# Hybrid decoder block: state blocks in pairs, four C products instead of two, normalised rows scaled later, parameters loaded as rows

## The chip, the cores and the metric

One core of a Trainium2 chip runs the whole program. The metric is the device time of one launch in microseconds (us). Engines are named as in the profile: PE (matrix engine; PEld its weight loads), DVE (vector), ACT (scalar), POOL (GpSimd), SP (sync, here only a DMA queue).

## The reference

One layer on 512 positions of width 1024. What matters here is the beginning:

```python
h = layer_norm(x, ln_in_g, ln_in_b)
proj = h @ w_in[l]
u, q, k, v, q_idx, k_idx, w_idx, gate_pre = jnp.split(proj, split_points, axis=-1)
...
dt = jnp.exp(log_dt)[:, None];  a_bar = jnp.exp(lam * dt)            # lam complex
bu = einsum('blgp,gnp->blgn', u, ((a_bar - 1.0) / lam)[..., None] * b_c)
_, states = lax.associative_scan(combine, (a_seq, bu), axis=1)       # s_t = a_bar s_(t-1) + bu_t
y = einsum('blgn,gpn->blgp', states, c_c).real + d_skip * u          # then GELU and a GLU
```

There are 32 groups of 16 channels with 64 complex states each. Beside this branch runs a sparse attention (an indexer picks 128 keys for each query, 8 heads). Both are gated and projected, added to the scaled h and normalised; then come the top 4 of 32 experts and a last normalisation.

## The kernel before

Each engine has a program of its own, written out by hand, and waits on semaphores; nothing is reordered. The time goes through these stages: a start (parameters and x are loaded, x is normalised and transposed), the first projection tiles, 16 state blocks on DVE with the other projection tiles on PE beside them, the indexer with its top-128 selection and the gates, the attention with the GLU, the output projection and the router, and the expert loop, which is about two thirds of the time.

**The start.** SP issues the loads of x (L379) and the weights of u (`chunk(0)`), then the small weights and `chunk(1)`. ACT's queue issues the parameters as columns, one number for each partition (L647 to L656), in its program *ahead of* the square roots of the first norm (L660); more parameters follow behind the square roots (L664 to L670). DVE normalises the four row tiles one after the other (L950 to L955, `norm`), PE transposes them (L1381), and ACT scales and shifts the transposed tiles into `hT` (L676). ACT and DVE then work out the coefficients of the states from `sp_in` (L680 to L686, L966 to L1003), and PE transposes the B and C blocks (L1432, L1439).

**Projection tiles.** A tile (`tile`, L1388 to L1420) is 8 fp32 matmuls of 512 columns, which the profile shows as 16 instructions (two passes each), into the PSUM banks 0 and 1 in turn; ACT takes it (`take`, L733). The four u tiles are done before the state blocks begin, 17 others (4 qi, ki, 4 q, 4 k, 4 v) beside them.

**State blocks.** Block j holds 128 states (two groups). For each of the 16: PE multiplies u by B into banks 2 and 3 (`bu`, L1452, contraction over 32 rows); ACT and POOL make the phase (`phase_products` on ACT, L475 to L486 on POOL) and ACT its sine and cosine (`trigs`, L702 to L704); DVE (`s5`, L1024 to L1049) rotates (4 products from PSUM, 2 sums), scans twice (L1037, L1038) and rotates back (4 products, L1044 and L1048 the difference and the sum) into `w_st`; PE multiplies by C (`ymm`, L1461, 32 output rows). Both `phase` and `w_st` have two buffers. Every fourth block DVE adds the skip term (`y_out`, L1055).

**What stands around it.** After the phases POOL multiplies and adds ln_in's rows to h (L504, L505: 8 instructions of 128x1024), which first the residual sum behind the output projection needs (semaphore `s_hrow`). Behind the last state block PE works out the indexer's head weights (L1481, semaphore `s_wi`), for which POOL and DVE wait before they split `hT` (L519, L1075); with these the gate tiles begin (L1494). In the attention POOL splits the GLU weights (L549, L551), and later w_o's (L558).

## Time and profile before

| | us |
|---|---|
| median of 3 runs | 1899.23 (1895.12 to 1900.89) |
| profiled execution, device time | 1896.33 |
| its span | 1894.5 |
| busy in the span: PE, DVE, ACT, POOL | 1712.5, 1550.2, 1078.5, 531.7 |
| share of PE on the chain that ended last | 72% |
| share of DVE on that chain | 18% |

Read the table with care: busy shares are means over stages with different limits. The chain of waits, followed in order of time, is what says who is last in each stage, and the table of busy times by stage says how full the others are. A PE instruction's duration holds its fill and drain; back to back matmuls overlap, so stretches are told from start to start.

### The profile page before, as it was taken

What the parts mean: (1) busy time and instruction counts of PE and PEld (TensorE: products, weight loads), DVE (VectorE), ACT (ScalarE), POOL (GpSimd) and SP (SyncE); (2) the same over time, 40 slices, a digit from 0 to 9 for tenths busy, and PEclk for the clock granted to TensorE, in tenths of its full rate; (3) what the DMA queues carried; (4) which work ended last, traced back from release to release, by engine and by line L of the source; (5) the groups of instructions that cost most, each with busy time, mean ns of one, the idle gap of its engine ahead of it and who ended that gap; (6) DMA issues with size and microseconds to landing.
All of it is one profiled execution on the core that took longest, in us unless ns stands there. A gap on an engine that the chain in (4) does not pass through costs nothing.

```text
span 1894.5 us, 22584 instructions
## 1 busy us (share of the span) xinstructions
PE 1712.5 (90%) x7162; PEld 1143.8 (60%) x7162; DVE 1550.2 (82%) x1738; ACT 1078.5 (57%) x1030; POOL 531.7 (28%) x310
## 2 busy tenths in 40 slices
PE   0899887798999768999999999999999999999992
PEld 0433333576666635777777777777777777777761
DVE  1399997794446777999999999999999999999993
ACT  0332321334544525777777777777777777777770
POOL 0165554435206235222222222222222222222220
PEclk9998997899999858999999999999999999999996
DMA  5120111112112366999999999999999999999973
GB/s 151 37 75 14 45 45 45 45 45 89 45 57 78 109 227 258 351 364 359 386 362 364 379 364 361 376 363 361 381 361 359 380 365 356 381 369 362 379 276 103
DMA packets 103796, 465.44 MB, mean 246 GB/s; under 512 B 33184, under 2 KB 33232, under 8 KB 54512
## 3 DMA queue, kind: packets, MB, share of 16 engines
q1 hardware_dynamic: 74064, 441.92, 61.1%
q0 software_dynamic: 9424, 16.86, 3.9%
q10 hardware_dynamic: 20272, 6.23, 1.4%
q8 instruction: 18, 0.29, 0.1%
q14 instruction: 18, 0.15, 0.0%
HBM read 454.81 MB, written 18.92 MB: 250 GB/s over the span
## 4 chain that ended last, share of the span: by engine, by line
PE 72%; DVE 18%; ACT 3%; issue 3%; ACTq 2%; POOL 1%; DMA 1%; DVEq 0%; POOLq 0%
PE ps L1668 19%; PE ps L1670 18%; PE ps L1669 18%; PE ps L1654 2%; PE ps L1419 2%; PE ps L1676 2%; PE ps L1414 2%; DVE scr L1037 1%; DVE scr L1038 1%; DVE scr L1093 1%; DVE top L1092 1%; DVE scr L1035 1%; PE ps L1524 1%; DVE scr L1034 1%; DVE scr L1042 1%
## 5 line engine op out<-in xcount | busy, mean ns | idle before, releaser
L1171 DVE TENSOR_TENSOR w_lo<-raw,w_hi 128x2048 fp32r<-128x2048 f32 x384 | 873.3, 2287 | 81.2 <-ACT w_hi L839 81.2
L839 ACT ACTIVATE w_hi<-raw 128x2048 fp32r<-128x2048 f32 x384 | 736.2, 1918 | 241.8 <-PE ps L1670 241.8
L1668 PE MATMUL ps<-w_hi,x_hi 128*96 128x512 f32 x1024 | 414.8, 405 | 0.0
L1669 PE MATMUL ps<-w_hi,x_lo 128*96 128x512 f32 x1024 | 402.8, 393 | 0.0
L1670 PE MATMUL ps<-w_lo,x_hi 128*96 128x512 f32 x1024 | 402.8, 393 | 0.0
L604 POOL DMA_INDIRECT gate_now<-gate_rows,row_now x32 | 80.2, 2506 | 468.7 <-DVE tok_out L1299 448.2
L1668 PE MATMUL ps<-w_hi,a_hi 128*96 128x512 f32 x512 | 204.2, 399 | 5.7 <-DVE a_lo L1270 5.7
L1670 PEld LDWEIGHTS ps<-w_lo,x_hi 128*96 128x96 f32 x1024 | 166.0, 162 | 70.9
L1668 PEld LDWEIGHTS ps<-w_hi,x_hi 128*96 128x96 f32 x1024 | 168.7, 165 | 65.6 <-issue 0.4
L1669 PEld LDWEIGHTS ps<-w_hi,x_lo 128*96 128x96 f32 x1024 | 166.6, 163 | 63.7
L1670 PE MATMUL ps<-w_lo,a_hi 128*96 128x512 f32 x512 | 202.2, 395 | 0.0
L1669 PE MATMUL ps<-w_hi,a_lo 128*96 128x512 f32 x512 | 201.7, 394 | 0.0
L612 POOL DMA_INDIRECT sum_rows<-far,tok_out x32 | 77.9, 2435 | 367.2 <-ACT far L927 367.2
L1419 PE MATMUL ps<-ring 128*128 128x512 f32 x256 | 126.5, 653 | 1.0 <-ACT ring L676 1.0
L1668 PEld LDWEIGHTS ps<-w_hi,a_hi 128*96 128x96 f32 x512 | 83.1, 162 | 39.3 <-issue 5.8
L1670 PEld LDWEIGHTS ps<-w_lo,a_hi 128*96 128x96 f32 x512 | 83.1, 162 | 36.2
L1669 PEld LDWEIGHTS ps<-w_hi,a_lo 128*96 128x96 f32 x512 | 83.3, 163 | 33.9
L1419 PEld LDWEIGHTS ps<-ring 128*128 128x128 f32 x256 | 52.5, 210 | 74.1 <-issue 72.7
L596 POOL DMA_INDIRECT scr<-h_rows,tok_now x33 | 72.1, 2184 | 80.4 <-DVE tok_now L1293 74.7
L1110 DVE SCALAR_TENSOR_TENSOR scr<-far,ps 128x128 f32<-128x128 f32 (+3 forms) x32 | 15.6, 488 | 62.9 <-PE ps L1524 61.8
L927 ACT ACTIVATE far<-ps,gate_now 96x512 f32<-96x512 f32 x64 | 40.3, 679 | 43.5 <-PE ps L1670 43.5
L1494 PE MATMUL ps<-hT_hi,wg_hi 128*128 128x512 f32 x128 | 52.1, 407 | 9.1 <-POOL wg_lo L515 9.1
(296 smaller groups left out, 2335.4 us busy)
## 6 DMA issues: line engine op xcount, KB each, us to landing
raw<-in_w_up SPq DMA_DIRECT2D x256, 1024.0 KB
raw<-in_w_down SPq DMA_DIRECT2D x128, 1024.0 KB
ring<-in_w_in SPq DMA_DIRECT2D x9, 2048.0 KB, 7.8
ring<-in_w_glu SPq DMA_DIRECT2D x4, 1024.0 KB, 6.2
ring<-in_w_o SPq DMA_DIRECT2D x2, 2048.0 KB, 11.9
h<-in_x SPq DMA_DIRECT2D x4, 512.0 KB, 5.6
ring<-in_w_attn_proj SPq DMA_DIRECT2D x1, 2048.0 KB, 9.1
h_rows<-h ACTq DMA_DIRECT2D x4, 512.0 KB
```

Source lines behind the costliest of these rows:

```text
L596: g.indirect_dma_start(xg[:, :], None, h1_rows, bass.IndirectOffsetOnAxis(ap=tok_now[:, 0:1], axis=0), bounds_check=last_tok, oob_is_err=F ...
L604: g.indirect_dma_start(gate_now[:, :], None, gate_rows, bass.IndirectOffsetOnAxis(ap=row_now[:, 0:1], axis=0), bounds_check=last_row, oob_ ...
L612: g.indirect_dma_start(sum_rows, bass.IndirectOffsetOnAxis(ap=tok_out[:, 0:1], axis=0), ysb.rearrange("p a b -> p (a b)"), None, bounds_ch ...
L839: s.activation(hi_of(c)[:, :], raw_of(c), ACT.Copy).then_inc(s_hi, 1)
L927: s.activation(ysb[:, r, :], ps[4 + r][0:BLK, :], ACT.Copy, scale=gate_now[:, 0:1]).then_inc(s_ysb, 1)
L1171: d.tensor_tensor(lo_of(c)[:, :], raw_of(c), hi_of(c)[:, :], ALU.subtract).then_inc(s_lo, 1)
L1414: ins = mm(o[:, :], w[:, k, P * i:P * i + P], qiT[:, k, :], start=k == 0, stop=k == 3)
L1419: ins = mm(o[:, :], w[:, k, c:c + P], hT[:, k, :], start=k == 0, stop=k == KD - 1)
L1494: mm(ps[n % 2][:, :], wg_hi[:, g % 2, k, :], hT_hi[:, k, :], start=k == 0, stop=False)
L1668: mm(o, xh, hi_of(c)[:, col], start=start, stop=False)
L1669: mm(o, xl, hi_of(c)[:, col], start=False, stop=False)
L1670: return mm(o, xh, lo_of(c)[:, col], start=False, stop=stop)
```

## The change

Four things change. (1) The parameters of one number for each partition are loaded as rows into `ptin` (84 rows of 128), spread by DVE for log_dt, transposed once by PE and copied to `ptab` by ACT. The loads of B, C, ln_in's rows and the router go from ACT's queue to SP's, behind `chunk(0)` and `chunk(1)`. The norm's measuring of tile t goes ahead of the shifting of tile t-1. (2) Only one u tile is made before the state blocks, three go into the stream of tiles beside them (20 tiles instead of 17). (3) `bu` and `ymm` take two blocks at a time, which lie in different groups of 32 rows (`bu`, four PSUM banks) or 32 output rows (`ymm`); `s5` leaves out the difference and the sum, and `ymm` multiplies the four products by C, -C' and so on, four matmuls for a block instead of two. `phase` has four buffers, `w_st` three. (4) POOL's 8 instructions on h go from behind the phases to behind the split of the GLU weights.

```diff
+        trig = scr[:, 0:4].rearrange("p (b r) t -> p b r t", b=2)
+        m = scr[:, 4:8]
+        phase, whole = v, ring[:, 4, 3136:3648]
+        part_lo = sb("part_lo", [P, SEQ])
+        rest = [ring[:, 5, 3584:4096], part_lo[:, :]]
+        w_st = [scr[:, 8:12], scr[:, 12:16], ring[:, 5, 1536:3584].rearrange("p (k t) -> p k t", k=4)]
...
+            for r, nm in enumerate(("b_re", "b_im")):
+                sp.dma_start(braw[:, r], a[nm][0].rearrange("(j w) n c -> (w n) j c", w=2)).then_inc(s_par[1], 16)
+            for r, nm in enumerate(("c_re", "c_im")):
+                src = a[nm][0].rearrange("(q g) c n -> (g c) q n", q=4)
+                for dup in range(2):
+                    sp.dma_start(craw[:, r, :, 64 * dup:64 * dup + 64], src).then_inc(s_par[2], 16)
...
+                if n == 1:
+                    for r, nm in enumerate(("ln_in_g", "ln_in_b")):
+                        sp.dma_start(gb[:, r, :], a[nm].partition_broadcast(P)).then_inc(s_gb1, 16)
+                    sp.dma_start(w_rt[:, :, :], a["w_router"][0].rearrange("(k p) n -> p k n", p=P)).then_inc(s_par[3], 16)
+                    sp.dma_start(b_rt[:, :], a["b_router"][0].partition_broadcast(P)).then_inc(s_par[3], 16)
...
-            pool.wait_ge(s_gb1, 32)
-            pool.wait_ge(s_lnT, KD)
-            for t in range(TT):
-                step(g.tensor_tensor(h[:, t, :], h[:, t, :], gb[:, 0, :], ALU.mult))
-                g.tensor_tensor(h[:, t, :], h[:, t, :], gb[:, 1, :], ALU.add).then_inc(s_hrow, 1)
-                pool.wait_ge(s_hrow, t + 1)
...
+            pool.wait_ge(s_gb1, 32)
+            pool.wait_ge(s_lnT, KD)
+            for t in range(TT):
...
+            for row, src in ((0, a["lam_re"][0].rearrange("(j w) n -> j (w n)", w=2)),
+                             (SJ, a["lam_im"][0].rearrange("(j w) n -> j (w n)", w=2)),
+                             (R_LN, a["ln_in_g"].rearrange("(k p) -> k p", p=P)),
+                             (R_LN + KD, a["ln_in_b"].rearrange("(k p) -> k p", p=P)),
+                             (R_GATE, a["b_gate"][0].rearrange("(k p) -> k p", p=P)),
+                             (R_SKIP, a["d_skip"][0].rearrange("(q g) c -> q (g c)", q=4))):
+                act.dma_start(ptin[row:row + src.shape[0], :], src).then_inc(s_ptl, 16)
+            act.dma_start(ldt[2 * SJ:3 * SJ, :], a["log_dt"][0].rearrange("(j w) -> j w", w=2)).then_inc(s_ptl, 16)
+            act.wait_ge(s_ptT, 1)
+            s.activation(ptab[:, :], ps[2][:, 0:NPAR], ACT.Copy).then_inc(s_ptab, 1)
...
+            act.wait_ge(s_ptab, 1)
+            s.activation(spw[:, 0, :], sp_in[:, 2, :], ACT.Exp).then_inc(s_dt, 1)
+            act.wait_ge(s_th, 1)
+            s.activation(spw[:, 2, :], spw[:, 1, :], ACT.Exp).then_inc(s_dt, 1)
             for k in range(KD):
                 act.wait_ge(s_lnT, k + 1)
                 s.activation(hT[:, k, :], ps[4 + k % 4][:, :], ACT.Identity, scale=gbc[:, 0, k:k + 1],
                              bias=gbc[:, 1, k:k + 1]).then_inc(s_hT, 1)
 
...
             def phase_products(j):
-                if j >= 1:
-                    act.wait_ge(s_ph, j)
                 if j >= 2:
-                    act.wait_ge(s_phfree, j - 1)
-                s.activation(phase[:, j % 2, :], tcol[:, :], ACT.Copy, scale=spw[:, 21, j:j + 1]).then_inc(s_prod, 1)
-                s.activation(turn[:, 1, :], tcol[:, :], ACT.Copy, scale=spw[:, 22, j:j + 1]).then_inc(s_prod, 1)
+                    act.wait_ge(s_ph, j - 1)
+                if j >= 4:
+                    act.wait_ge(s_phfree, j - 3)
+                s.activation(phase[:, j % 4, :], tcol[:, :], ACT.Copy, scale=spw[:, 21, j:j + 1]).then_inc(s_prod, 1)
+                s.activation(rest[j % 2], tcol[:, :], ACT.Copy, scale=spw[:, 22, j:j + 1]).then_inc(s_prod, 1)
             def trigs(j):
-                if j + 1 < SJ:
-                    phase_products(j + 1)
+                if j + 3 < SJ:
+                    phase_products(j + 3)
                 act.wait_ge(s_ph, j + 1)
                 if j >= 2:
-                    act.wait_ge(s_rot, j - 1)
-                s.activation(trig[:, j % 2, 1, :], phase[:, j % 2, :], ACT.Sin, scale=TWO_PI).then_inc(s_trig, 1)
-                step(s.activation(trig[:, j % 2, 0, :], phase[:, j % 2, :], ACT.Abs))
+                    act.wait_ge(s_st, j - 1)
+                s.activation(trig[:, j % 2, 1, :], phase[:, j % 4, :], ACT.Sin, scale=TWO_PI).then_inc(s_trig, 1)
...
+            act.wait_ge(s_tau, 1)
+            act.wait_ge(s_const, 2)
+            phase_products(0)
+            phase_products(1)
+            take(n)
+            n += 1
+            phase_products(2)
+            for q in range(8):
+                act.wait_ge(s_bbT, q + 1)
+                r, qq = q // 4, q % 4
+                s.activation(bT[:, r, qq, :], ps[4 + q % 4][:, 0:P], ACT.Copy).then_inc(s_bT, 1)
...
+            def measure(t):
+                dve.wait_ge(s_x[t], 16)
+                for r in range(2):
+                    step(d.bn_stats(stats[:, r, :], h[:, t, 512 * r:512 * r + 512]))
+                d.bn_aggr(mvx[:, t, :], stats[:, :, :]).then_inc(s_var, 1)
+                dve.wait_ge(s_var, t + 1)
+
+            def shift(t):
+                dve.wait_ge(s_rstd, t + 1)
+                step(d.reciprocal(rsx[:, t, 1:2], rsx[:, t, 0:1]))
+                d.tensor_scalar(h[:, t, :], h[:, t, :], mvx[:, t, 0:1], rsx[:, t, 1:2], ALU.subtract, ALU.mult)\
+                    .then_inc(s_xhat, 1)
+
+            dve.wait_ge(s_ptl, 7 * 16)
+            d.tensor_copy(ptin[2 * SJ:3 * SJ, :].rearrange("j (w n) -> j w n", w=2),
+                          ldt[2 * SJ:3 * SJ, :].unsqueeze(2).to_broadcast([SJ, 2, STATES])).then_inc(s_ptx, 1)
             for t in range(TT):
-                dve.wait_ge(s_x[t], 16)
-                norm(h[:, t, :], t + 1, step).then_inc(s_xhat, 1)
-                dve.wait_ge(s_xhat, t + 1)
+                measure(t)
+                if t > 0:
+                    shift(t - 1)
+            shift(TT - 1)
...
-                if j >= 2:
-                    dve.wait_ge(s_stfree, j - 1)
-                wr, w_im = w_st[:, j % 2, 0, :], w_st[:, j % 2, 1, :]
-                step(d.tensor_tensor(m[:, 0, :], m[:, 1, :], c, ALU.mult))
-                step(d.tensor_tensor(m[:, 2, :], m[:, 3, :], sn, ALU.mult))
-                step(d.tensor_tensor(wr, m[:, 0, :], m[:, 2, :], ALU.subtract))
-                step(d.tensor_tensor(m[:, 0, :], m[:, 1, :], sn, ALU.mult))
-                d.tensor_tensor(m[:, 2, :], m[:, 3, :], c, ALU.mult).then_inc(s_rot, 1)
-                dve.wait_ge(s_rot, j + 1)
-                d.tensor_tensor(w_im, m[:, 0, :], m[:, 2, :], ALU.add).then_inc(s_st, 1)
+                if j >= 3:
+                    dve.wait_ge(s_stfree, (j - 3) // 2 + 1)
+                w = w_st[j % 3]
+                step(d.tensor_tensor(w[:, 0, :], m[:, 1, :], c, ALU.mult))
+                step(d.tensor_tensor(w[:, 1, :], m[:, 3, :], sn, ALU.mult))
+                step(d.tensor_tensor(w[:, 2, :], m[:, 1, :], sn, ALU.mult))
+                d.tensor_tensor(w[:, 3, :], m[:, 3, :], c, ALU.mult).then_inc(s_st, 1)
                 dve.wait_ge(s_st, j + 1)
 
             def y_out(q):
-                dve.wait_ge(s_stfree, 4 * q + 4)
...
+            pe.wait_ge(s_ptx, 1)
+            tr(ps[2][:, 0:NPAR], ptin[0:NPAR, :], ident[0:NPAR, 0:NPAR]).then_inc(s_ptT, 1)
...
-            def bu(j):
-                rows = slice(32 * (j % 4), 32 * (j % 4) + 32)
-                if j >= 1:
-                    pe.wait_ge(s_bufree, j)
+            def bu(p):
+                if p % 2 == 0:
+                    pe.wait_ge(s_tile_a, p // 2 + 1)
+                if p >= 1:
+                    pe.wait_ge(s_bufree, 2 * p)
                 for r in range(2):
-                    ins = mm(ps[2 + r][:, :], bT[rows, r, j // 4, :], uT[rows, j // 4, :], start=True, stop=True)
+                    for j in (2 * p, 2 * p + 1):
+                        rows = slice(32 * (j % 4), 32 * (j % 4) + 32)
+                        ins = mm(ps[2 + 4 * (j % 2) + r][:, :], bT[rows, r, j // 4, :], uT[rows, j // 4, :], start=True,
+                                 stop=True)
                 ins.then_inc(s_bu, 1)
-            def ymm(j):
-                q, rows = j // 4, slice(32 * (j % 4), 32 * (j % 4) + 32)
-                pe.wait_ge(s_st, j + 1)
-                if j % 4 == 0 and q > 1:
+            def ymm(p):
+                q = p // 2
+                pe.wait_ge(s_st, 2 * p + 2)
+                if p % 2 == 0 and q > 1:
                     pe.wait_ge(s_yfree, q - 1)
-                for r in range(2):
-                    ins = mm(ps[5 - q % 2][rows, :], cblk[:, r, j, :], w_st[:, j % 2, r, :], start=r == 0, stop=r == 1)
+                for k, r in enumerate((0, 2, 1, 1)):
+                    for j in (2 * p, 2 * p + 1):
+                        rows = slice(32 * (j % 4), 32 * (j % 4) + 32)
+                        ins = mm(ps[5 - q % 2][rows, :], cblk[:, r, j, :], w_st[j % 3][:, k, :], start=k == 0, stop=k == 3)
                 ins.then_inc(s_stfree, 1)
-            order = [(1, 4), ("small", 1), (2, 4), (3, 4), (4, 4)]
-            flat = [(c, i == cnt - 1) for c, cnt in order for i in range(cnt)]
-            for j, (c, last) in enumerate(flat):
-                if j < SJ:
-                    bu(j)
+            order = [(0, 3), (1, 4), ("small", 1), (2, 4), (3, 4), (4, 4)]
+            flat = [c for c, cnt in order for i in range(cnt)]
+            bu(0)
+            for i, c in enumerate(flat):
                 if c == "small":
                     pe.wait_ge(s_small, 32)
-                elif c != (flat[j - 1][0] if j else None):
+                elif c != (flat[i - 1] if i else 0):
                     arrive(c)
                 tile(n, c if c != "small" else 0)
                 n += 1
-                if 1 <= j <= SJ:
-                    ymm(j - 1)
+                if i % 2 == 0 and 1 <= i // 2 <= SJ // 2:
+                    ymm(i // 2 - 1)
+                if i % 2 == 1 and i // 2 + 1 < SJ // 2:
+                    bu(i // 2 + 1)
+            pe.wait_ge(s_bufree, SJ)
```

## Rows read from the trace of the kernel before

**Rows 1.** Stages: length; PE, PEld, DVE, ACT, POOL busy; granted clock; DMA; GB/s

```profile
0.00:38.70 38.70, 0.00 (x0) 0.00 (x0) 1.74 (x6) 0.00 (x0) 1.84 (x8) 1.00 0.67 179
...
38.70:61.60 22.90, 8.12 (x33) 6.47 (x33) 8.69 (x17) 7.96 (x14) 0.00 (x0) 1.00 0.44 86
...
61.60:97.60 36.00, 35.27 (x86) 16.01 (x87) 12.12 (x41) 11.64 (x26) 9.23 (x9) 0.99 0.08 24
...
97.60:281.70 184.10, 167.44 (x346) 61.70 (x345) 177.47 (x197) 50.06 (x84) 104.23 (x83) 0.94 0.12 41
...
281.70:304.40 22.70, 13.31 (x27) 4.20 (x25) 22.32 (x13) 2.95 (x5) 22.09 (x8) 0.87 0.00 1
...
319.10:339.70 20.60, 14.01 (x76) 11.08 (x77) 11.30 (x11) 6.94 (x7) 9.59 (x4) 0.66 0.29 102
...
455.50:564.70 109.20, 102.44 (x507) 75.76 (x507) 49.41 (x114) 57.24 (x120) 27.96 (x29) 0.97 0.13 46
```

**Rows 2.** Start in order of time (start, duration, engine)

```profile
38.73 1.28 ACT L660 ACT_TABLE_LOAD   x1 [38.73 <-issue]
...
40.35 0.16 DVE L953 RECIPROCAL rstd<-rstd 128x1 f32<-128x1 f32 x1 [34.50 <-ACT rstd L660]
...
43.42 0.16 DVE L953 RECIPROCAL rstd<-rstd 128x1 f32<-128x1 f32 x1 [0.36 <-ACT rstd L660]
...
53.84 0.53 ACTq L668 DMA_DIRECT2D gb<-in_ln_in_g  x1
```

**Rows 3.** DMA issues until 100 us: KB each, us to landing

```profile
ring<-in_w_in SPq DMA_DIRECT2D x3, 2048.0 KB, 12.7
...
h<-in_x SPq DMA_DIRECT2D x4, 512.0 KB, 5.6
...
bgate<-in_b_gate ACTq DMA_DIRECT2D x1, 8.0 KB, 3.6
```

**Rows 4.** Last normalised tile to first state block, in time order

```profile
49.77 0.81 DVE L955 TENSOR_SCALAR h<-h,mv,rstd 128x1024 f32<-128x1024 f32 x1
...
56.08 5.46 ACT L676 ACTIVATE ring<-ps,gbc 128x512 f32<-128x512 f32 x8 [6.55 <-issue]
...
61.59 16.32 PE L1419 MATMUL ps<-ring 128*128 128x512 f32 x32 [1.00 <-ACT ring L676]
...
65.59 0.20 DVE L980 TENSOR_TENSOR spw<-spw 128x16 f32<-128x16 f32 x1 [0.21 <-ACT spw L686]
...
74.52 0.91 DVE L1009 MEMSET ring<- 128x1024 f32 x1 [0.28 <-issue]
...
97.60 0.69 DVE L1029 TENSOR_TENSOR scr<-ps,scr 128x512 f32<-128x512 f32 x1 [17.36 <-ACT scr L704]
```

**Rows 5.** DVE groups, first 14 state blocks: count, busy us, mean ns

```profile
L1037 DVE TENSOR_TENSOR_SCAN scr<-spw,scr 128x512 f32<-128x512 f32 x14 | 22.0, 1572 | 0.5
...
L1044 DVE TENSOR_TENSOR scr<-scr 128x512 f32<-128x512 f32 x14 | 10.6, 760 | 0.5
...
L1029 DVE TENSOR_TENSOR scr<-ps,scr 128x512 f32<-128x512 f32 x14 | 9.7, 691 | 17.7 <-ACT scr L704 17.4
```

**Rows 6.** A scan without POOL beside it, on DVE

```profile
312.22 1.22 DVE L1037 TENSOR_TENSOR_SCAN scr<-spw,scr 128x512 f32<-128x512 f32 x1
```

**Rows 7.** PE and its weight loads (PEld), in order of time

```profile
117.90 7.13 PE L1419 MATMUL ps<-ring 128*128 128x512 f32 x16
...
319.12 1.90 PE L1461 MATMUL ps<-scr,ring 128*32 128x512 f32 x4 [0.26 <-DVE scr L1048]
...
319.57 0.11 PEld L1461 LDWEIGHTS ps<-scr,ring 128*32 128x32 f32 x1 [0.32 <-issue]
...
320.95 9.53 PE L1481 MATMUL ps<-ring 128*128 128x8 f32 x64
...
346.81 0.70 PE L1507 MATMUL ps<-kiT,qiT 64*128 64x256 f32 x4
```

**Rows 8.** POOL between the GLU weights and w_o, in order of time

```profile
568.63 2.61 POOL L558 TENSOR_TENSOR wo_lo<-ring,wo_hi 128x512 fp32r<-128x512 f32 x2 [67.04 <-ACT wo_hi L830]
```

More of the change, by code:

```diff
@@ L478, in _ @@
                 tau = spw[:, 20, j:j + 1]
[L479 to L480 removed]
+                f, r = phase[:, j % 4, :], whole
+                lo = rest[j % 2]
                 step(g.tensor_scalar(r, tcol[:, :], tau, ROUND, ALU.mult, ALU.add))
@@ L1443, in _ @@
-            pe.wait_ge(*taken[n - 1])
+            tile(n, 0)
+            n += 1
+            pe.wait_ge(s_par[2], 64)
+            for r in range(2):
+                for q in range(4):
+                    tr(ps[2 + r][:, P * q:P * q + P], craw[:, r, q, :], ident[:, :]).then_inc(s_cT, 1)
+            pe.wait_ge(s_bb, 1)
+            for q in range(8):
+                r, qq = q // 4, q % 4
+                if q >= 4:
+                    pe.wait_ge(s_bT, q - 3)
+                tr(ps[4 + q % 4][:, 0:P], bblk[:, r, 4 * qq:4 * qq + 4, :].rearrange("p j c -> p (j c)"), ident[:, :])\
+                    .then_inc(s_bbT, 1)
```

107 lines of the change are left out of this document (29 added, 78 removed).

## Prediction

> **What bounds the kernel now.** I read the table of stages first, then the chain of waits in order of time, then the timelines where the chain changes engine. Of the 1894.5 us the change touches the first 340 and one place in the attention. In those 340 there are four stages.
>
> From 0 to 38.7 nothing computes: PE, DVE and ACT are busy 0, 1.74 and 0 us [rows 1]. ACT's queue is issuing DMAs, and the square root stands behind them in ACT's program, so that even its table load begins at 38.73. DVE waited 34.5 us for the root [rows 2]. x was there long before (5.6 us to landing) [rows 3].
>
> From 38.7 to 97.6 the path is: four norm tiles on DVE, the transposes, then ACT, which came to the first `hT` tile at 56.08 only, since its queue was issuing again; two u tiles on PE in 16.32 us; B and C; two more u tiles; and the first state block at 97.60, for which DVE waited 17.36 us [rows 4]. PE is busy 35.27 of 36.0 us from 61.6 on [rows 1].
>
> From 97.6 to 319.1 the chain is DVE's: 177.47 busy of 184.1 us for the first 14 blocks, the rest the gaps between instructions [rows 1]. PE is nearly as full, 167.44, but waits for DVE. From 281.7 to 304.4 POOL's 8 instructions on h run (22.09 us busy), and DVE gets only 13 instructions done in 22.7 us [rows 1].
>
> From 319.1 on: the last C product 1.90 us, the indexer's weights 9.53 us on PE, and at 330.5 POOL and DVE begin to split `hT` [rows 7]. From there to the attention the change alters no instruction. I take 330.5 as the post at which the stages are compared.
>
> **Part 1, the start.** ACT's queue now issues 7 DMAs of a few long rows. Neighbours of few large pieces cost it 0.53 us each [rows 2], so 7 x 0.53 = 3.7, and the last is issued at 4.5. To landing: 3.6 us in a quiet queue for bgate, 5.6 for x's 512 KB [rows 3]. I take 3.8, nearer the first since the pieces are small: 8.3. The ends are 7 and 15.5, the latter if the rows wait until u's weights are in (issued at 2.8, 12.7 to landing) [rows 3]. DVE, which waits for these rows ahead of its first norm, has behind it: the spreading, 0.3 (estimate), and four norm tiles. The distance of two reciprocals is 3.07, of which 0.36 is the wait for the root [rows 2], which measuring ahead hides: 4 x 2.7 = 10.8. The last tile is normalised at 19.4. PE's transpose of the parameters and ACT's copy lie inside that.
>
> Before, the last tile was normalised at 50.6 [rows 4] and the eight `hT` tiles ended at 61.5, held up by ACT. Without that hold PE's transposes set the pace: 32 of them and a first one kept PE busy for 8.12 us [rows 1], and all but the first three stand behind the last normalised tile: 29 x 0.246 = 7.1, and ACT's last copy 0.5 (5.46 for 8 [rows 4], partly beside it). `hT` is ready at 27. Now two strands run. PE: the first u tile takes 16.32 - 7.1 = 9.2 (the second runs at 7.1 [rows 7], the first partly at half the rate) and ends at 36.4. DVE: from the sines to the B blocks 65.6 to 74.3, 8.7 us [rows 4]; the sines come behind `hT` with a table load of 1.28 and 0.7 us of small work: 27 + 2.0 + 8.7 = 37.7. Then C's blocks: a clearing of 1.5 times 0.91 [rows 4], six copies at 0.45: 42 with a little contention, and C's transposes are done by then. The B products of the first pair, 2 to 2.5 us: DVE starts block 0 at 45. The phases are ready a little before, at 44: ACT's products at 31, two turns of POOL at 5 to 6 us each, then cosine and sine. B, C and the small weights, now on SP's queue behind `chunk(0)`, hold up nothing: SP computes nothing, `chunk(1)` behind them is needed at 70, and B at 33. **97.6 to 45 is 52.6 us less**; range 48 to 57.
>
> **Part 2, the state blocks.** A product of two tiles takes 691 ns [rows 5], and the gap behind each instruction is (184.1 - 177.47) / 197 = 0.034 [rows 1]: 0.726. A scan alone takes 1.22, so 1.26 [rows 6]. A block by itself: 12 x 0.726 + 2.52 = 11.2. Measured: 184.1 us for 14 blocks and two skip terms, less one instruction, so 13.1. The 1.85 between is POOL's doing: the scans' mean is 1572 ns here, the sum's 760, while products that read PSUM keep 691 [rows 5]. The new block has 10 instead of 12: 16 x (10 x 0.726 + 2.52) = 156.5. POOL's work on the phases stays; some 14 of 16 phases fall beside the blocks: 14 x 1.85 = 25.9. Three skip terms, 2.3. Together 184.7 against 221.5: **36.8 us less**, of which 23.2 are the 32 instructions left out and 12 the removal of POOL's work on h. Does PE keep up? For a pair: 2 tiles 14.3, `bu`, `ymm`. Two matmuls of 64 rows each in different row groups, four passes of 256 columns, took 0.70 us [rows 7]; one after the other four such passes would be 4 x 0.21 + 0.27 = 1.1 (a tile's 16 passes of 512 columns take 7.13, 0.43 to 0.45 each [rows 7]). So row groups do run side by side here, and `bu` costs about 2. For output column groups no row of the trace shows it. `ymm` has 16 passes: 3.7 if pairs overlap, 7.0 if not (4 took 1.90 [rows 7]). PE then has 20.0 or 23.3 at full clock against DVE's 184.7 / 8 = 23.1. Granted clock was 0.94 [rows 1], which makes the tiles some 0.5 to 0.8 longer: 21.3 or 24.6. I take the overlapping, by the nearest row. `bu` of the next pair may be 4 us late before DVE notices, since six instructions of the last block run on behind its release. End of block 15: 45 + 184.7 = 229.7, ends 181 and 198 for the stage.
>
> The Trainium skill ("TensorE: Matmul & The Clock Gate", Part 3: Packing small matmuls) states a measured speedup of 2.38 for three column groups of 32 at 512 columns; by it two would take hardly more than one, an estimate of 3.7 to 4.2 for `ymm`. The same part says that a weight load overlaps a running matmul only when the row groups differ, which speaks against `ymm`, where they are the same. The trace disagrees: L1461's weight loads (0.11 us) fall into the stretch of its four matmuls, and these took no longer than passes of a tile, 4 x 0.43 and a drain [rows 7]. By the rule a pair would cost 16 x 0.11 = 1.8 us more on PE, which the slack above just holds.
>
> **Part 3, what comes back behind the blocks.** Before, `ymm` of the last block and the weights followed at once. Now the stream has 20 tiles, and three of them stand behind the last `ymm` in PE's program. PE can't do them earlier, as it waits there for DVE. Behind block 15: 3.7 + 3 x 7.13 + 9.53 = 34.7 against 11.4 [rows 7], and 1 for a clock that falls while PE waits: **24 us more**, ends 22 and 28. ACT's copy of `hT` waits for the last of these tiles too, but its 3.6 us lie beside the 9.53. So of the 23 us that the three u tiles saved ahead of the blocks, the tail takes nearly all back.
>
> **Part 4, POOL's work on h.** It moves to where POOL was idle for 67.04 us [rows 8]; about 22 us fit in ahead of w_o, and neither ACT's nor DVE's wait on `s_hrow` is last there. DVE is busy 49.41 of 109.2 us in this stage and PE 102.44 [rows 1], so what POOL slows on DVE is mostly hidden. One instruction in twelve there reads two tiles of SBUF, and could take 2 us longer, two or three times: 0 to 5, I take 1. On SP's and ACT's queues nothing else is moved past a wait.
>
> **The sum.** The profiled execution took 1896.33, its span 1894.5, and it lies 2.9 below the median. -52.6 - 36.8 + 24 + 1 = -64.4, so 1832 for an execution like the profiled one, and 1834.8 from the median 1899.23. I give 1834.
>
> **Rivals.** (A) Column groups don't overlap, so the change does not do that part of what it says. PE needs 24.6 us for a pair against 23.1: 8 x 1.5 = 12, and 3.3 at the tail, and as PE no longer waits there is no slack for slow tiles: 3 more. 1852. For it: no row shows column groups. Against: row groups do overlap. Chance 0.12. (B) The clock falls more often: PE now waits in one piece a pair, with the small `bu` behind it; in the stage where it waited most before (13.31 busy of 22.7 us) the granted clock was 0.87 against 0.94 [rows 1]. With tiles of 10 a pair takes 25.7: 8 x 2.6 = 21. 1855. Against: a slower PE waits less, which brings the clock back. 0.13. (C) The parameter rows land only with u's weights at 15.5: +7, 1841. 0.10. (D) Slower than before: PE stays at the lower of its two levels, 1.2 GHz, through the blocks, as it was most of the time from 319.1 to 339.7 (0.66 [rows 1]). Tiles of 14.3, `bu` and `ymm` doubled: 40 us for a pair, 8 x 17 = 136, and 25 at the tail: 1995. It decides once a tile is x longer with 8 x (2x - 3.1) + 3x = 65, where 3.1 is PE's slack in a pair and 65 my gain: x = 4.7, a tile of 11.9. The granted clock of 0.94 with PE busy for 91% of the stage [rows 1] speaks against it. 0.03. (E) POOL's phases, made ahead, disturb DVE half as much: 13 less, 1821. 0.04.
>
> **How the numbers follow.** My forecast has 0.58: 1824 to 1845 by its own bounds. C and E lie at its rim. A and B reach to 1856. 1820 to 1857 leaves out D and some of A and B, under 2 in 10. 0.3% (5.7 us) is about what a measurement of this kernel tells from no change; only D is slower: faster 0.96, same 0.01, slower 0.03.
>
> **What would show it.** The first square root at about 10 us and block 0 at 45: part 1. DVE without waits from there to 230 and ten instructions a block: part 2; waits of DVE for `bu` mean A or B, and `ymm` of 3.7 or 7.0 us tells which. Three v tiles between the last `ymm` and L1481's successor: part 3. The attention within 5 us of 109: part 4. Wrong would make it a wait that I don't see between the pairs, or a start that hangs on B's landing.

## The result, and the profile of the changed kernel

| | before | after |
|---|---|---|
| median, us (4 runs each, same chip) | 1900.06 (1895.12 to 1904.45) | 1841.82 (1839.94 to 1844.39) |
| ratio, with its 95% interval | | 0.9691 (0.9673 to 0.9709) |
| profiled execution; its span | 1896.33; 1894.5 | 1839.94; 1838.2 |

The kernel is 3.1% faster, some 58 us. The forecast was 1834, from 1820 to 1857. The time lies inside, 8 us above the likeliest value. The stages of the two profiled executions show where these 8 come from.

One line from the top of the changed kernel's page (busy time, share of the span and instructions of each engine):

```profile
PE 1696.1 (92%) x7227; PEld 1139.8 (62%) x7227; DVE 1519.6 (83%) x1709; ACT 1081.0 (59%) x1032; POOL 524.9 (29%) x310
```

Its stages, cut where the work changes (columns as in [rows 1]: length; PE, PEld, DVE, ACT, POOL busy; granted clock; DMA share; GB/s). They are the start until ACT's first square root, the rest of the start, the state blocks, what PE does behind them, the gap before the gate tiles, the first 6.1 us of the gate tiles, and the attention. The rest of the gate tiles (285.0 to 393.6) and all behind 506.6 are left out:

```profile
0.00:10.97 10.97, 0.37 (x1) 0.18 (x1) 2.33 (x8) 2.81 (x4) 1.84 (x8) 1.00 0.84 317
10.97:49.70 38.73, 19.83 (x73) 11.62 (x73) 26.13 (x60) 19.49 (x39) 21.25 (x20) 0.86 0.51 140
49.70:232.00 182.30, 167.94 (x436) 64.27 (x437) 173.21 (x195) 50.60 (x85) 88.43 (x72) 0.94 0.12 42
232.00:269.70 37.70, 37.70 (x136) 22.01 (x134) 2.20 (x9) 7.78 (x7) 0.61 (x1) 0.88 0.22 79
269.70:278.90 9.20, 2.60 (x9) 1.19 (x9) 9.13 (x4) 1.04 (x3) 9.01 (x3) 0.50 0.00 1
278.90:285.00 6.10, 6.10 (x15) 4.81 (x16) 3.08 (x3) 1.67 (x2) 2.35 (x1) 0.51 0.00 0
393.60:506.60 113.00, 103.62 (x513) 76.31 (x512) 53.24 (x120) 59.99 (x125) 49.78 (x40) 0.97 0.14 48
```

[rows 1] cuts the attention of the kernel before at 455.5. From the same instruction as here, its first matmul (L1524 before, L1552 now), it is:

```profile
452.50:564.70 112.20, 103.28 (x513) 76.27 (x512) 50.85 (x120) 60.09 (x125) 30.49 (x32) 0.97 0.14 49
```

Set against [rows 1], with the attention cut in this way, this gives the account of the span. The start takes 49.7 instead of 97.6 us (-47.9, forecast -52.6), the blocks 182.3 instead of 221.5 (-39.2, forecast -36.8), and from the last block to the split of `hT` it takes 37.7 instead of 11.5 (+26.2, forecast +24). From the split of `hT` to the attention it takes 1.9 more, the attention 0.8 more (forecast 1), and what follows 1.8 more, which is less than single executions differ by. The sum is -56.4. The spans differ by 56.3.

**The start**, DVE in order of time:

```profile
8.64 0.22 DVE L979 COPY ptin<-ldt 16x128 f32<-16x128 f32 x1 [7.58 <-DMA ldt<-in_log_dt]
...
18.65 0.81 DVE L975 TENSOR_SCALAR h<-h,mvx,rsx 128x1024 f32<-128x1024 f32 x1
...
29.40 1.10 DVE L1012 TENSOR_TENSOR spw<-spw,ptab 128x16 f32<-128x16 f32 x1
30.54 0.17 DVE L1013 TENSOR_TENSOR spw<-spw,ptab 128x16 f32<-128x16 f32 x1
...
34.83 0.42 DVE L1023 TENSOR_TENSOR scr<-spw,far 128x256 f32<-128x256 f32 x1
35.29 1.37 DVE L1024 TENSOR_TENSOR scr<-spw,far 128x256 f32<-128x256 f32 x1
...
49.73 0.69 DVE L1053 TENSOR_TENSOR scr<-ps,scr 128x512 f32<-128x512 f32 x1 [3.98 <-PE ps L1474]
```

Three things are to be seen. The wait for the last parameter row ends at 8.64; before, 34.5 us went to waiting for the root [rows 2]. Instructions of one form last 0.17 or 1.10 us, and 0.42 or 1.37. Block 0 waits for PE at the end. PE in the same stretch:

```profile
25.91 7.13 PE L1441 MATMUL ps<-ring 128*128 128x512 f32 x16 [1.81 <-ACT ring L688]
...
41.34 1.97 PE L1459 MATMUL ps<-ident,far 128*128 128x128 f32 x8 [7.43 <-DVE far L1027]
45.85 3.78 PE L1474 MATMUL ps<-uT,ring 32*128 32x512 f32 x8 [2.54 <-issue]
```

PE stands for 7.43 us in front of the B blocks and then does the first B products in 3.78 us, at a granted clock of 0.50 (1.2 GHz) from 45.8 to 49.6. The second pair, at 65.06 with a granted clock of 1.00, takes 1.99.

**The blocks**, DVE by groups (count | busy us, mean ns | idle before). The products that read PSUM kept their 691 ns; what reads two tiles of SBUF, and the scans, take longer on the mean than alone (0.69 and 1.22 us):

```profile
L1062 DVE TENSOR_TENSOR_SCAN scr<-spw,scr 128x512 f32<-128x512 f32 x16 | 23.5, 1466 | 0.6
L1061 DVE TENSOR_TENSOR_SCAN scr<-spw,scr 128x512 f32<-128x512 f32 x16 | 21.4, 1335 | 0.5
L1058 DVE TENSOR_TENSOR scr<-scr 128x512 f32<-128x512 f32 x16 | 13.7, 859 | 0.5
...
L1054 DVE TENSOR_TENSOR scr<-ps,scr 128x512 f32<-128x512 f32 x16 | 11.1, 691 | 0.5
```

The waits of PE in the blocks (us in total, times, longest):

```profile
PE ps L1474 <- DVE scr L1056: 12.8, 5, 4.0
```

And the first passes of the C products of a pair of blocks on PE, in order of time. The two blocks write different column groups, each its own 32 of the 128 output rows (`ring` and `scr` are their two `w` buffers):

```profile
101.41 0.62 PE L1487 MATMUL ps<-ring 128*32 128x512 f32 x1
101.42 0.62 PE L1487 MATMUL ps<-scr,ring 128*32 128x512 f32 x1
101.87 0.59 PE L1487 MATMUL ps<-ring 128*32 128x512 f32 x1
...
104.97 5.42 PE L1441 MATMUL ps<-ring 128*128 128x512 f32 x12
```

Both passes of a pair start within 0.01 us, the next pair 0.43 later, and the next tile starts 3.56 us behind the first: `ymm` costs 3.6, as forecast for column groups side by side.

**Behind the blocks**, PE:

```profile
234.10 0.62 PE L1487 MATMUL ps<-ring 128*32 128x512 f32 x1
...
237.66 20.87 PE L1422 MATMUL ps<-ring 128*128 128x512 f32 x48
258.36 11.28 PE L1509 MATMUL ps<-ring 128*128 128x8 f32 x64
```

Three tiles stand between `ymm` and the indexer's weights, as forecast.

### The profile page after: what moved, and what is told of

The parts are those of the page before. It is cut to its first block, busy times and chain, and to the rows that moved or that the text cites. A ratio compares the mean times of both kernels' runs of the same rounds, so it can differ in the third digit from the quotient of the medians.

```text
span 1838.2 us, 22681 instructions
## 1 busy us (share of the span) xinstructions
PE 1696.1 (92%) x7227; PEld 1139.8 (62%) x7227; DVE 1519.6 (83%) x1709; ACT 1081.0 (59%) x1032; POOL 524.9 (29%) x310
## 4 chain that ended last, share of the span: by engine, by line
PE 77%; DVE 14%; issue 3%; ACT 3%; DMA 1%; POOL 1%; ACTq 0%; DVEq 0%; POOLq 0%
PE ps L1696 19%; PE ps L1698 19%; PE ps L1697 19%; PE ps L1682 3%; PE ps L1441 2%; PE ps L1704 2%; PE ps L1436 2%; PE ps L1422 2%; DVE scr L1112 1%; DVE top L1111 1%; DVE scr L1062 1%; PE ps L1552 1%; PE ps L1430 1%; DVE scr L1061 1%; PE ps L1571 1%
```

## The experiments

All are the changed kernel with one edit, unless said otherwise; ratios are to the kernel before on the same chip. The runs used three chips, on which the kernel before took 1897.9 (e1 to e4), 1904.2 (e5, e7 to e9) and 1902.5 us (e10, e11), so a difference of a few us between two medians is better read from the ratios. My theory has four parts. The start is worth its 48 us, most of it from the way in which the parameters are loaded. The blocks gain by shorter work of DVE, whose instructions POOL stretches. Column groups overlap, but PE's share is slack. And the u tiles saved ahead of the blocks return behind them.

### e1: POOL's scaling of h back beside the blocks

```
 # POOL, ahead of  pool.wait_ge(s_far0, 1)
+            pool.wait_ge(s_gb1, 32)
+            pool.wait_ge(s_lnT, KD)
+            for t in range(TT):
+                step(g.tensor_tensor(h[:, t, :], h[:, t, :], gb[:, 0, :], ALU.mult))
+                g.tensor_tensor(h[:, t, :], h[:, t, :], gb[:, 1, :], ALU.add).then_inc(s_hrow, 1)
+                pool.wait_ge(s_hrow, t + 1)
 # and the same lines taken out beside the attention
```

> The changed kernel with POOL's 8 instructions on h put back behind the phases, beside the last state blocks. My theory: they cost DVE 12 us there and about 1 in the attention, so 11 us more than the changed kernel's 1842: 1853, and DVE's scans beside them take over 3 us. Rival: PE, not DVE, sets the end of the last blocks by now, which swallows most of it: 1845 or less. Second rival: in the attention they cost as much as in the blocks: 1842.

1855.01 us (1854.19 to 1857.08), ratio 0.9763 (0.9733 to 0.9794). The blocks (columns as in the stages above):

```profile
51.30:248.39 197.09, 174.41 (x432) 66.53 (x433) 187.05 (x195) 50.72 (x85) 109.22 (x80) 0.87 0.10 35
```

The same 195 instructions of DVE are busy for 13.8 us more than in the changed kernel (173.2), while POOL works 20.8 us more beside them, and the stage is 14.8 longer. The place of POOL's work is worth 13 us of the whole. How it comes about is seen where one scan stands beside it; the first line is POOL's, the second DVE's:

```profile
202.53 2.68 POOL L525 TENSOR_TENSOR h<-h,gb 128x1024 f32<-128x1024 f32 x1
203.03 3.26 DVE L1061 TENSOR_TENSOR_SCAN scr<-spw,scr 128x512 f32<-128x512 f32 x1
```

While POOL's last five instructions on h follow each other, from 202.5 to 217.1, DVE gets five instructions done, of 2.65 to 3.26 us each (alone 0.69 or 1.22), about one for each of POOL's. What it costs beside the attention can't be read: the attention takes 115.6 us here, without POOL's work on h in it, 113.0 in the changed kernel, and 112.4 to 116.1 in the traces of the other experiments, all of which have it there.

### e2: two C products, sum and difference on DVE again

```
-                for k, r in enumerate((0, 2, 1, 1)):
+                for k, r in enumerate((0, 1)):
 # and on DVE, per block
+                step(d.tensor_tensor(w[:, 0, :], m[:, 0, :], m[:, 2, :], ALU.subtract))
...
+                d.tensor_tensor(w[:, 1, :], m[:, 0, :], m[:, 2, :], ALU.add).then_inc(s_st, 1)
```

> The changed kernel with the difference and the sum back on DVE (12 products and sums a block instead of 10) and two C products a block on PE, still in pairs. My theory: DVE bounds the blocks, so 32 x 0.726 = 23 us more there and 2 less for the shorter last C product: 1863. Rival: PE bounds the blocks nearly as much (it waits only 13 us in them), so that leaving out the 32 instructions was worth 12 us or less, and this comes out at 1852 to 1854.

1863.48 us (1859.3 to 1865.13), ratio 0.9812 (0.9781 to 0.9843).

```profile
50.32:256.30 205.98, 168.25 (x384) 65.19 (x384) 196.57 (x227) 51.66 (x86) 86.55 (x72) 0.85 0.12 41
```

DVE does 32 instructions more and is busy for 23.4 us more; the stage grows by 23.7. `ymm` is halved (eight passes, the next tile 1.84 us behind the first), and that saves nothing in the blocks, where DVE does more at the same time: PE's waits for DVE grow from 12.8 to 29.4 us. The two additions left out are worth their whole time on DVE.

### e3: C products of a pair block after block

```
-                for k, r in enumerate((0, 2, 1, 1)):
-                    for j in (2 * p, 2 * p + 1):
-                        rows = slice(32 * (j % 4), 32 * (j % 4) + 32)
+                for j in (2 * p, 2 * p + 1):
+                    rows = slice(32 * (j % 4), 32 * (j % 4) + 32)
+                    for k, r in enumerate((0, 2, 1, 1)):
```

> The changed kernel with the C products of a pair issued block after block, all four of one and then all four of the other, so that neighbouring matmuls share their 32 output columns. My theory: ymm takes 7.0 instead of 3.6 us; PE then has over 23.3 us for a pair against DVE's 23: 8 to 12 us more in the blocks and 3.4 behind them, 1853 to 1857. Rival: PE's slack takes it in and only the 3.4 us behind the last block show: 1845. Second rival: the order doesn't matter for the overlap and nothing changes: 1842.

1844.87 us (1843.62 to 1852.09), ratio 0.9724 (0.9688 to 0.976): less than the loss expected. By the medians it is 3 us slower than the changed kernel, by the ratios 6; the intervals of the two overlap. `ymm` did not take 7.0 us:

```profile
100.95 2.33 PE L1487 MATMUL ps<-ring 128*32 128x512 f32 x5
102.70 0.62 PE L1487 MATMUL ps<-scr,ring 128*32 128x512 f32 x1
103.12 0.59 PE L1487 MATMUL ps<-ring 128*32 128x512 f32 x1
...
106.25 1.98 PE L1441 MATMUL ps<-ring 128*128 128x512 f32 x4
```

While the last passes of the first block run, the second block's already go beside them, although they stand behind in the program. `ymm` takes 5.3 us, so half of the overlap is kept. The blocks were 7.4 us longer (last product at 239.56 from block 0 at 50.59; before this edit 231.31 from 49.73), but not by the reason I had given, PE's lack of slack. No wait of DVE for PE appears behind block 0, and PE still waited 7.8 us for DVE. DVE's own instructions were stretched, the scans to 1813 and 1614 ns on the mean:

```profile
L1061 DVE TENSOR_TENSOR_SCAN scr<-spw,scr 128x512 f32<-128x512 f32 x15 | 27.2, 1813 | 0.5
```

180.2 us busy instead of 173.2, for the same 195 instructions. The number is that of the first rival (1845), but not its reason: the stretch behind the blocks did not grow by 3.4 us, it was 36.0 instead of 37.7. I took it that POOL's turns fall differently on DVE's instructions. This called for a kernel without POOL's turns (e7) and for the same order in it (e10).

### e4: four u tiles ahead of block 0

```
 # PE, ahead of the transposes of the B blocks
+            tile(n, 0)
+            n += 1
 # PE, behind them
+            for _ in range(2):
+                tile(n, 0)
+                n += 1
-            order = [(0, 3), (1, 4), ("small", 1), (2, 4), (3, 4), (4, 4)]
+            order = [(1, 4), ("small", 1), (2, 4), (3, 4), (4, 4)]
```

> The changed kernel with all four u tiles ahead of the state blocks as before (one of them where PE waits for the B blocks) and 17 tiles in the stream. Theory of the prediction: moving u tiles into the stream gave ahead of the blocks about what it took behind them; with one tile now in PE's idle 7.4 us and two that delay the blocks by 14.3, against three tiles of 7.1 less behind them and 2 us less at the low clock: 14.3 - 21.4 - 2 = -9, so 1833. Rival: the moved tiles are a net gain of the change and this is slower, 1849 (14.3 less 7.1).

1831.7 us (1827.22 to 1835.08), ratio 0.9648 (0.9616 to 0.968): faster than the changed kernel, by 10 us in the medians and 8 by the ratios. PE at the start and behind the blocks:

```profile
37.75 3.60 PE L1444 MATMUL ps<-ring 128*128 128x512 f32 x8
41.93 1.53 PE L1465 MATMUL ps<-ident,far 128*128 128x128 f32 x8 [0.58 <-DVE far L1030]
...
57.13 1.99 PE L1483 MATMUL ps<-uT,ring 32*128 32x512 f32 x8
```

```profile
249.16 8.82 PE L1518 MATMUL ps<-ring 128*128 128x8 f32 x64
```

Block 0 starts at 60.97, 11.2 later; the split of `hT` at 258.07, 11.7 earlier. The three tiles cost 11 ahead of the blocks, and the stretch behind them is 23 shorter (14.5 instead of 37.7), 2.5 of that in the indexer's weights. One of the three fills the 7.43 us in which PE stood idle, and it keeps the clock up (the B blocks' transposes take 1.53 instead of 1.97, the first B products 1.99 instead of 3.78). The indexer's weights take 8.82 instead of 11.28. The three u tiles saved ahead of the blocks are a loan that the tail takes back, and one of them costs extra.

### e5: parameters as columns again

```
 # ACT's queue
-                act.dma_start(ptin[row:row + src.shape[0], :], src).then_inc(s_ptl, 16)
+            act.dma_start(sp_in[:, 0, :], a["lam_re"][0].rearrange("(j w) n -> (w n) j", w=2)).then_inc(s_ptl, 16)
...
+            act.dma_start(gbc[:, 0, :], a["ln_in_g"].rearrange("(k p) -> p k", p=P)).then_inc(s_ptl, 16)
```

> The changed kernel with the parameters loaded as columns again (8 DMAs on ACT's queue, one number for each partition; B, C and the rest stay on SP's queue; no transpose of the rows). My theory: issuing them holds ACT's queue as before, some 33 to 38 us to the first square root instead of 11, and the first state block comes 24 to 27 us later: 1866 to 1869. Rival: the gain at the start came from taking B's and C's loads off ACT's queue and from measuring ahead, the shape of the parameter loads is hidden: 1850 or less.

1867.64 us (1867.19 to 1871.63), ratio 0.9823 (0.9791 to 0.9856). DVE's wait for the first root, which had vanished, is back:

```profile
39.77 0.16 DVE L974 RECIPROCAL rsx<-rsx 128x1 f32<-128x1 f32 x1 [31.85 <-ACT rsx L680]
```

Block 0 starts at 77.95 instead of 49.73, 28.2 later, and the blocks behind are what they were (181.9). Of the 47.9 us at the start, 28 are thus the issue of scattered words on ACT's queue, until 38.05 here. The other 20 are what is left of the start: three u tiles fewer ahead, B, C and the router's weights off this queue, and the order of the work. No run separates these.

### e7: without POOL's rounding of the phases

```
-                step(g.tensor_scalar(r, tcol[:, :], tau, ROUND, ALU.mult, ALU.add))
-                step(g.tensor_scalar(r, r, ROUND, None, ALU.subtract))
-                step(g.tensor_tensor(f, f, r, ALU.subtract))
-                step(g.tensor_tensor(f, f, lo, ALU.add))
```

> The changed kernel without 4 of POOL's 5 instructions on each phase (the rounding to whole turns and the two differences are left out, the clamp stays). My theory: POOL's instructions are what stretches DVE's blocks from 9.8 to some 11.6 us, 26 us in all. Without them DVE needs 157 us for the blocks, and PE, with 20 us for a pair, becomes the bound at 160 to 166: 16 to 20 us less, 1822 to 1826, the scans at 1.22 us each. Rival: DVE's excess is its own (its reads and writes of SBUF), and neither the scans nor the time change: 1842.

1815.25 us (1813.91 to 1817.57), ratio 0.9542 (0.9511 to 0.9573), 27 under the changed kernel and 7 below the lower end of what I expected. This kernel leaves part of the phases out, so it shows what that work costs and is no candidate.

```profile
46.79:210.20 163.41, 160.07 (x439) 62.15 (x440) 154.73 (x195) 50.59 (x85) 15.41 (x23) 0.98 0.14 49
210.20:244.80 34.60, 34.60 (x133) 19.62 (x131) 2.23 (x8) 7.78 (x7) 0.61 (x1) 0.93 0.21 74
```

```profile
L1057 DVE TENSOR_TENSOR_SCAN scr<-spw,scr 128x512 f32<-128x512 f32 x16 | 21.0, 1314 | 0.5
L1058 DVE TENSOR_TENSOR_SCAN scr<-spw,scr 128x512 f32<-128x512 f32 x16 | 20.5, 1280 | 0.6
...
L1054 DVE TENSOR_TENSOR scr<-scr 128x512 f32<-128x512 f32 x16 | 11.1, 692 | 0.5
```

The numbers are four lines lower than in the changed kernel: L1057 is L1061 there, L1058 is L1062, L1054 is L1058. The same 195 instructions are 154.7 us busy instead of 173.2. So POOL's rounding of the phases cost DVE 18.5 us in the blocks, for 73 us of POOL's own work. At the start too: L1024's counterpart takes 0.43 instead of 1.37, and block 0 starts 2.9 us earlier. PE is now busy for 160 of 163 us. And the tail is 34.6 us instead of 37.7: PE comes 1.0 us late to the last `ymm` instead of 2.1, and the indexer's weights take 9.31 instead of 11.28.

The Trainium skill ("SBUF — State Buffer", Who interferes with whom) says that a DVE instruction with two SBUF inputs contends with a GpSimd instruction that reads SBUF, and that one with at most one SBUF input doesn't, outside of certain modes. The traces agree with both halves: 691 ns for the products that read PSUM with and without POOL, and 859 against 692 for the first sum of two SBUF tiles (L1058).

### e10: e3's order in e7

> Like e7 it leaves out POOL's rounding of the phases (four instructions of each phase), so part of the computation is changed; and like e3 it issues the C products of a pair block after block. What is tested: why e3's blocks were 7.4 us longer. In e3 no wait of DVE for PE appears, and DVE's own instructions were busy for 180.0 us instead of 173.2 (scans 1813 and 1614 ns instead of 1466 and 1335), so my theory is that the longer C products cost nothing directly there, since PE had slack, and that the 7 us came from how POOL's turns fell on DVE's. In e7 PE is busy for 160.1 of 163.4 us, so its slack is gone: C products longer by 1.8 us in each of 8 pairs must now show in full as waits for PE, about +11 to +14 us in the blocks, and the time goes from e7's 1815 to 1826 to 1829. Rival: PE still has slack or DVE stays last, the order costs under 4 us here: 1815 to 1819.

1825.27 us (1822.75 to 1826.03), ratio 0.9593 (0.9569 to 0.9616), 10 more than e7 and just under the 1826 to 1829 expected. The blocks and the stretch to the split of `hT`:

```profile
45.32:211.52 166.20, 166.20 (x427) 62.76 (x428) 154.20 (x195) 50.62 (x85) 13.19 (x23) 0.99 0.11 38
211.52:253.60 42.08, 42.08 (x145) 22.98 (x143) 2.24 (x9) 7.78 (x7) 0.62 (x2) 0.93 0.28 100
```

PE has no idle time left in the blocks (166.20 of 166.20), and DVE's busy time is that of e7 (154.2): without POOL's turns the order stretches nothing. Of the 10.3 us by which block 0 to `hT` is longer than in e7, only 2.8 lie in the blocks, where DVE's waits for ACT grow from 2.2 to 5.5 us; ACT copies out PE's tiles in between its sines. 7.5 lie behind them: PE comes 6.0 us late to the last `ymm` instead of 1.0, `ymm` itself takes 1.7 more, the indexer's weights 0.7. I had expected all of it in the blocks, as waits of DVE for PE. So the overlap of column groups is worth some 10 us once PE is the bound, here for half of it; in the changed kernel PE was not, and there e3's loss of 3 to 6 us came with a DVE stretched by 7.0. That the stretching is gone together with POOL's rounding bears out POOL as its cause.

### e8: a u tile in PE's idle stretch, C's blocks ahead

```
 # PE, ahead of the transposes of the B blocks
+            tile(n, 0)
+            n += 1
-            order = [(0, 3), (1, 4), ("small", 1), (2, 4), (3, 4), (4, 4)]
+            order = [(0, 2), (1, 4), ("small", 1), (2, 4), (3, 4), (4, 4)]
 # and C's transposes and blocks moved ahead of `hT` on PE and ahead of the sines on DVE
```

> The changed kernel with a second u tile where PE waits 7.4 us for the B blocks, and with C's transposes ahead of the first tile, and its blocks and both clearings on DVE in the 6.3 us in which DVE waits for the sines. My theory: the tile costs nothing there and takes 7.1 from behind the blocks; it also keeps PE's clock up, so the first B products take 2 instead of 3.8; the C blocks' 4 us and 0.9 of clearing leave the path: block 0 at 43 instead of 49.7, in all 7.1 + 6.5 = 13 to 14 us less, 1828. Rival: ACT, which also makes the phases, holds block 0 at 46 or later: 1832 to 1835.

1833.3 us (1828.83 to 1837.18), ratio 0.9643 (0.9611 to 0.9675). The B products are done at 45.6, but block 0 waits for ACT:

```profile
47.15 0.69 DVE L1054 TENSOR_TENSOR scr<-ps,scr 128x512 f32<-128x512 f32 x1 [5.50 <-ACT scr L712]
```

Block 0 starts 2.6 us earlier with two tiles done in place of one, the split of `hT` at 260.27 (269.73). The gain of 8.5 us is made up of 2.6 at the start and 9.4 in the tail (28.3 instead of 37.7: one tile less, and 8.79 for the indexer's weights), less 2.5 by which the blocks are longer, with DVE busy for 178.2. The rival (ACT holds block 0) was the right one.

### e9: e8, and two v tiles in PE's slack between the blocks

```
+                k = i - (i > 7) - (i > 14)
+                if i in (7, 14):
+                    continue
 # ACT
-                take(n)
+                for _ in range(2 if j in (8, 14) else 1):
+                    take(n)
```

> The kernel of e8_tile_and_c_early with the last two v tiles moved from behind the last C product into the stream, one ahead of the fifth pair and one ahead of the eighth. My theory: PE waits some 13 us for DVE in the blocks, and a B product may come 4 us late unnoticed, so 14.3 us leave the tail and 0 to 5 come back as waits of DVE: 10 to 14 less than the kernel of e8, about 1816. Rival: the slack is spent on tiles at the low clock already, DVE waits for what PE does more, and nothing is gained over the kernel of e8.

1821.85 us (1819.92 to 1828.59), ratio 0.9573 (0.9543 to 0.9603): 4.3% under the kernel before and 1.1% under the changed one, the fastest that leaves nothing out. PE behind the blocks:

```profile
227.38 14.00 PE L1429 MATMUL ps<-ring 128*128 128x512 f32 x32
241.31 0.62 PE L1492 MATMUL ps<-ring 128*32 128x512 f32 x1
...
244.87 9.37 PE L1517 MATMUL ps<-ring 128*128 128x8 f32 x64
```

No tile is left behind `ymm`. But DVE waited 3.4 us for PE between the blocks, was busy 179.6 us instead of 173.2, and PE came 5 us late to the last `ymm`. The split of `hT` at 254.33 is 5.9 us earlier than in e8, not 14. The medians of e8 and e9 differ by 11.5, inside the 10 to 14 that I expected (though not at 1816), but the traces show only these 5.9, and the two profiled executions took the same time (1828.8 and 1828.6): how much of the 11.5 the two tiles gave isn't settled.

### e11: e9, sine and cosine of block 0 earlier on ACT

```
             phase_products(2)
+            trigs(0)
             for q in range(8):
                 act.wait_ge(s_bbT, q + 1)
```

> e9 with ACT's three instructions for the sine and cosine of block 0 moved ahead of its eight copies of the B blocks, into a stretch where ACT idled for 5.9 us; the products of phase 3 stay behind. Theory: block 0 then waits for PE's B products alone, which end at about 45.6, so it starts at 45.6 to 45.9 instead of 46.8 to 47.2, and the rest is as in e9: 1820 to 1821.5 against e9's 1821.85, under what the times can tell, so the start of block 0 in the profile decides. Rival: POOL's turns fall on other instructions of DVE, and the blocks get 3 to 7 us longer or shorter by that, as between e8, e9 and the kernel after (178.2, 179.6 and 173.2 us busy for the same 195 instructions); then the gain is lost in it, 1815 to 1828.

1823.7 us (1820.68 to 1827.79), ratio 0.9581 (0.9558 to 0.9605), no difference from e9 that can be measured. Block 0 does start earlier, at 45.16, waiting for PE's B products alone. But the blocks are 1.2 us longer than in e9 (190.8 against 189.6), with DVE busy for 180.3 us and a wait of 4.0 us for PE at 216.48, where e9 has one of 3.4. The last `y` is written 0.4 us earlier, and then the indexer's weights take 11.7 us instead of 9.4, so that `hT` is split at 256.26. So the start moved as the theory said and the gain was lost behind it, as the rival had it, though half in another place: in the time of the indexer's weights on PE.

## Why the prediction was right, point by point

**Part 1, the start: right in mechanism, 4.7 us too good.** The last parameter row was there at 8.64 (forecast 8.3), the last tile normalised at 19.46 (19.4), and `hT` stood ready at 25.9 (27). The first u tile needed 7.13, not 9.2. The sines were there at 27.9 instead of 29.0. The step that failed is DVE's 8.7 us from there to the B blocks, which I had taken from [rows 4], where POOL had only begun its turns. Now POOL's first phases run beside it and it took 13.4 (27.86 to 41.28), 4.7 more. e7 shows it: without POOL's rounding the same stretch takes 9.0 (29.37 to 38.35). From the B blocks to block 0 it was 1.2 more than forecast, 1.0 of it in the last step: `bu` of the first pair took 3.78 at half clock where I had 2 to 2.5. PE had stood for 7.43 us ahead of the transposes and 2.54 behind them, waits that I had not followed. The long one isn't needed for it; in e7 the two were 2.98 and 2.69:

```profile
38.41 1.81 PE L1455 MATMUL ps<-ident,far 128*128 128x128 f32 x8 [2.98 <-DVE far L1023]
...
42.92 3.78 PE L1470 MATMUL ps<-uT,ring 32*128 32x512 f32 x8 [2.69 <-issue]
```

Rival C, rows that land late, did not occur. e5 puts 28 of the 48 us on ACT's queue.

**Part 2, the blocks: right, 2.4 us too cautious.** Ten instructions for a block, and DVE without waits except for ACT's 2.6 us and block 0: 182.3 against 184.7. The 23.2 us for the 32 instructions were 23.7 (e2), the 12 for POOL's work on h were 14.8 (e1). The term that was mis-sized is POOL's excess, 1.85 for each of 14 blocks, 25.9. Without it DVE's 195 instructions would be busy for some 151.8 us (160 of 0.69, 32 scans of 1.22, 3 skip terms of 0.75); they were for 173.2, so it is 21.4, of which the rounding makes 18.5 (e7). The 2.9 left in e7, where POOL still clamps the phases, no run divides. Against it stands the wait of 2.6 for ACT, which the sum did not have. The column groups overlap (3.6 us), so rival A is out, and the clock stayed at 0.94 as before, so B and D are out. E had half of POOL's excess in view, 13 us less; it came to 4.5 less.

On the rule of the Trainium skill weighed there ("TensorE: Matmul & The Clock Gate", Part 3: Packing small matmuls): its speedup for column groups is borne out for two groups, 3.56 us for 16 passes where one by one, at 0.43 each, would be 7.0. Its sentence that a weight load overlaps only when the row groups differ is not: the passes of a pair use the same rows, three more weight loads of 0.11 us start at 101.42 to 101.45 while the pass of 101.41 runs, and the passes stay 0.43 us apart.

**Part 3, the tail: right, 2.2 us too good.** 3.6 + 20.7 + 11.3 and 2.1 us in which PE was still at a tile when the last block ended (232.0 against 234.1). I had 9.53 and 1 for the weights, by [rows 7]; they took 11.28 at a granted clock of 0.62; those of [rows 7] ran at 0.75. Over the traces the same 64 matmuls took from 8.5 (e5) to 11.7 us (e11), and what sets it is open. The claim that the tail takes nearly all of the start's three tiles back is what e4 shows, and more: with them ahead the kernel is 8 to 10 us faster.

**Behind it, 1.9 us that I had not counted.** The gate tiles start on a slow clock in both kernels, but stay on it longer now: 15 passes in 6.1 us, shown above at 0.51, against 20 in 6.1 us of the kernel before, from its first gate tile:

```profile
339.70:345.80 6.10, 6.07 (x20) 4.92 (x21) 3.12 (x3) 1.67 (x2) 2.39 (x1) 0.75 0.02 4
```

Five passes at 0.43 are 2.1 us. Why the clock rose later is not settled; PE stood for 6.13 us in front of them, and for 6.07 in the kernel before. It isn't a price of the change either: from the split of `hT` to the attention the traces of the experiments have 121.2 to 126.6 us, with the same instructions, and 122.0 before and 123.9 now lie in that.

**Part 4: right, as far as it can be read.** The attention is 0.8 us longer, less than it varies from trace to trace (e1), with 19.3 us of POOL's work on h around its middle (8 instructions from 442.9 to 462.8, of which the four additions are):

```profile
L572 POOL TENSOR_TENSOR h<-h,gb 128x1024 f32<-128x1024 f32 x4 | 9.9, 2463 | 0.3
```

The same work cost 13 us beside the blocks (e1), where DVE is last.

**The sum was closer than its terms.** The blocks were 2.4 us better than forecast, the start 4.7 and the tail 2.2 worse, and in the blocks an excess sized 4.5 too high covered a wait of 2.6 that was not in the sum. That these cancel in part is luck.

**Left open.** How POOL's turns come to fall on DVE's instructions. The same 195 instructions were busy for 173.2, 178.2 (e8), 179.6 (e9), 180.2 (e3) and 180.3 us (e11). Beside them stood 72 instructions of POOL in the changed kernel and in e3, and 75 or 76 in the others, which at e7's rate (18.5 us of DVE for 73 of POOL) are worth about 1 us. No experiment set the order by itself.

## What to carry to other kernels

Where DVE sets the pace, first take away what POOL does beside its instructions with two SBUF inputs: 20 us of POOL's work cost 13 beside the blocks, and in the attention, where PE is busy for 103.6 of 113.0 us, too little to be read. Work of PE that is taken from ahead of a DVE-bound stretch comes back behind it unless it is spread into PE's waits; follow the tiles to the end of the program, and put one wherever PE stands idle, for the clock falls there as well. An overlap on an engine that has slack gains nothing there until the slack is gone (halving the C products in e2 saved nothing in the blocks; half of the overlap was worth 10 us in e10).
